# A streaming encoder layer: projecting all tiles first, and mixing with the output projection between its steps

## What is computed

```python
def trunk_layer(x, c, S0, k_cache, v_cache, lb, ...):
    mod = jnp.dot(jax.nn.silu(c), w_ada) + b_ada              # 9 rows of 6 x 1024
    sh1, sc1, g1, sh2, sc2, g2 = [m[:, None, :] for m in jnp.split(mod, 6, axis=-1)]
    h = rmsnorm(x, ln1) * (1 + sc1) + sh1
    qa, ka, va, qb, fb, ib, gb = jnp.split(jnp.dot(h, w_in), SPLITS, axis=-1)
    # widths 512, 128, 128, 512, 512, 512, 512
    # A: QK norm per head, windowed attention (8 heads, 2 key heads) with sinks and ALiBi -> oa
    # B: HGRN2 recurrence over blocks, 8 heads of a 64 x 64 state:
    #    logf = log sigmoid(z), k = sigmoid(-z), b = cumsum(logf)
    #    o = tril((q k) exp(b_t - b_s)) i + (q exp(b)) S,  S' = exp(b_last) S + (k exp(b_last - b))^T i
    ob = rmsnorm(ob, o_norm) * jax.nn.silu(gb)
    x = x + g1 * jnp.dot(jnp.concatenate([oa, ob], axis=-1), w_out)
    h2 = rmsnorm(x, ln2) * (1 + sc2) + sh2
    x = x + g2 * moe(h2, ...)                                 # 16 experts, top 2
```

## Time and profile before

| | us |
|---|---|
| median of 3 runs (lowest, highest) | 1480.14 (1477.21, 1480.64) |
| the profiled execution's own time | 1478.23 |
| its span | 1476.5 |
| PE busy in the span | 1276.9 |
| DVE, ACT, POOL busy | 771.5, 545.0, 264.5 |
| mean granted PE clock | 0.914 |

### The profile page before, as it was taken

How to read it: one execution, slowest core, us unless ns; L and a number is a source line. 1 busy time by engine, 2 the same in 40 slices (tenths; PEclk the granted TensorE clock), 3 DMA queues, 4 the chain that set the end, 5 groups by cost and what they waited for, 6 DMA issues and landing times. The chain is left out here.

```text
span 1476.5 us, 21409 instructions
## 1 busy us (share of the span) xinstructions
PE 1276.9 (86%) x6661; PEld 919.6 (62%) x6662; DVE 771.5 (52%) x1187; ACT 545.0 (37%) x916; POOL 264.5 (18%) x287
## 2 busy tenths in 40 slices
PE   5529999999999999994969973699999999969964
PEld 0014666665766666564648863588888787858853
DVE  0010656466475655647244446555528665865752
ACT  0011535435253443524143330444416444644540
POOL 1000101102010110204000000233133233323313
PEclk7759999999999999995779995799999999989988
DMA  9970000000000000005273328458667979898874
GB/s 355 415 286 11 5 15 0 14 0 14 14 0 14 0 14 0 14 2 130 38 202 124 118 100 291 151 182 273 215 184 250 332 256 309 300 309 253 266 281 85
DMA packets 87921, 215.01 MB, mean 146 GB/s; under 512 B 16577, under 2 KB 20289, under 8 KB 84818
## 3 DMA queue, kind: packets, MB, share of 16 engines
q1 hardware_dynamic: 75794, 170.58, 32.3%
q0 software_dynamic: 12096, 44.05, 11.4%
HBM read 188.31 MB, written 26.23 MB: 145 GB/s over the span
## 5 line engine op out<-in xcount | busy, mean ns | idle before, releaser
L481 PE MATMUL psum<-w_in_sb,x_res 128*128 128x512 f32 (+1 forms) x864 | 353.2, 563 | 4.4 <-DVE x_res L471 4.4
L481 PEld LDWEIGHTS psum<-w_in_sb,x_res 128*128 128x128 f32 x864 | 160.9, 191 | 164.1 <-issue 156.8
L1942 PE MATMUL psum<-e_w_h,e_x_h 128*128 128x512 f32 x432 | 174.9, 405 | 29.5 <-DVE w_gu L2055 23.1
L1943 PE MATMUL psum<-w_gu,e_x_h 128*128 x432 | 171.8, 398 | 0.0
L1944 PE MATMUL psum<-e_w_h,e_x_l 128*128 128x512 f32 x432 | 171.6, 397 | 0.0
L2055 DVE TENSOR_TENSOR w_gu<-w_gu,e_w_h 128x1024 f32 x128 | 146.7, 1220 | 20.5 <-ACT e_w_h L1996 20.5
L1996 ACT ACTIVATE e_w_h<-w_gu 128x1024 fp32r x128 | 123.0, 1048 | 53.9 <-issue 33.0
L1889 POOL DMA_INDIRECT out<-e_work,e_to x26 | 87.6, 3371 | 302.3 <-DVE e_work L2043 302.3
L1942 PEld LDWEIGHTS psum<-e_w_h,e_x_h 128*128 128x128 f32 x432 | 83.4, 193 | 47.9 <-DVE w_gu L2055 23.6
L1944 PEld LDWEIGHTS psum<-e_w_h,e_x_l 128*128 128x128 f32 x432 | 83.3, 193 | 18.2
L1943 PEld LDWEIGHTS psum<-w_gu,e_x_h 128*128 128x128 f32 x432 | 83.4, 193 | 17.0
(11 more groups left out here) (393 smaller groups left out, 2055.9 us busy)
## 6 DMA issues: line engine op xcount, KB each, us to landing
w_gu<-in_w_e_gate SPq DMA_DIRECT2D x16, 2048.0 KB, 11.0
w_gu<-in_w_e_up SPq DMA_DIRECT2D x16, 2048.0 KB, 15.8
w_dn<-in_w_e_down SPq DMA_DIRECT2D x16, 2048.0 KB, 15.2
stage<-in_w_ada SPq DMA_DIRECT2D x24, 1024.0 KB, 13.2
x_res<-in_x SPq DMA_DIRECT2D x20, 512.0 KB, 3.7
w_in_sb<-in_w_in SPq DMA_DIRECT2D x5, 2048.0 KB, 19.0
out<-r_x SPq DMA_DIRECT2D x9, 512.0 KB, 2.6
h_d<-r_h SPq DMA_DIRECT2D x9, 512.0 KB, 2.9
```

Source lines behind the costliest of these rows:

```text
L481: last = pe.matmul(psum[:, PJ0 + j % 2, 0:n], h_t[:, k, :], b["w_in_sb"][:, k, a:a + n], start=(k == 0), stop=(k == KC - 1))
L1942: pe.matmul(psum[:, j, :], x_h[:, k, :], wh, start=(k == 0), stop=False)
L1943: pe.matmul(psum[:, j, :], x_h[:, k, :], wl, start=False, stop=False)
```

## The change

The stages become projection, sampling, mixing, routing, experts; `output` is gone as a stage.

**Projection** makes h for all nine tiles, split in a high and a low part (`h_h`, `h_l`) that stay in SBUF, and walks over `w_in` by column group, each group loaded and split once (ACT high, DVE low, two slots), for all tiles. A job is one group for one tile, 24 fp32r products; for f and q the weights are the stationary operand, so the result comes out with features on partitions, 128 features by 384 rows a job. The elementwise work follows each job and the results go to memory (`feat` 9.4 MB: running sum, log key less running sum, key, query; `tok` 8.3 MB: i, gate, q, k, v). `w_ada` chunks 8 to 23 are loaded and used between jobs.

```diff
+GROUPS = (("i", CIB, QW), ("f", CFB, QW), ("q", CQB, QW), ("kv", CK, 2 * KW), ("qa", CQ, QW), ("g", CGB, QW))
+BY_WEIGHT = ("f", "q")
+JOBS = [(g, n) for g, (name, _, _) in enumerate(GROUPS) for n in range(4 * NCH if name in BY_WEIGHT else NT)]
+BANKS = 4
+STAGES = 3
+TOK_RING = 3
...
+            for n, (g, i) in enumerate(JOBS):
...
+                if name == "i":
+                    if i + 1 < NT:
+                        turn_x(i + 1)
+                    pe.wait_ge(s["hl_ready"], i + 1)
...
+                    if name in BY_WEIGHT:
...
+                        pe.matmul(out, wh, h_h[:, k, at], start=(k == 0), stop=False)
+                        pe.matmul(out, wl, h_h[:, k, at], start=False, stop=False)
+                        last = pe.matmul(out, wh, h_l[:, k, at], start=False, stop=(k == KC - 1))
...
+                if name in BY_WEIGHT and i < KC:
...
+                    ada(chunk)
+            def load_x(t):
+                if t >= 2:
+                    sp.wait_ge(s["x_turned"], t - 1)
...
+                if name == "i":
+                    if i + 2 < NT:
+                        load_x(i + 2)
```

**Sampling** comes before the mixing, reads the ninth tile from memory, and loads and splits `w_out`:

```diff
+            for kv in range(NKV):
+                sp.dma_start(w_raw[kv * HD:(kv + 1) * HD, 0:G, :],
...
+            sp.dma_start(w_raw[:, G:KC, :], d["w_out"][QW:2 * QW, :]...
...
+            def split(ks):
+                act.wait_ge(s["w_out_loaded"], 3 * 16)
+                for k in ks:
+                    a(w_oh[:, k, :], w_raw[:, k, :], ACT.Copy).then_inc(s["wh_ready"], 1)
...
             act.wait_ge(s["kgap_ready"], 1)
             a(k_d[:, :], k_d[:, :], ACT.Exp).then_inc(s["kexp_ready"], 1)
+            split(range(0, 2))
             act.wait_ge(s["top_ready"], 2)
```

**Mixing** is an unrolled loop over eight tiles, which loads each tile's `feat` and `tok` (double-buffered). POOL makes the gaps:

```diff
+                pool.tensor_tensor(g[:, :, 0, :], e[:, :, 0, :], mid, ALU.add)
+                pool.tensor_tensor(g[:, :, 1, :], c[:, :, 1, :], mid, ALU.subtract).then_inc(s["gap_ready"], 1)
...
+                pool.tensor_tensor(xw[:, :], x2[:, u % 2, :], table_row(2, u), ALU.mult).then_inc(s["xw_ready"], 1)
```

PE's order has six fp32r products of the output projection of the tile before (`fill`) in the places of the projection:

```diff
+                fill(t, 0)
+                scores(t, 0)
+                level(t, 0)
+                if t:
+                    turn_ob(t - 1)
+                fill(t, 1)
+                level(t, 1)
+                if t:
+                    pe.wait_ge(s["mixb_ready"], t)
+                    turn_h2(t - 1)
+                fill(t, 2)
+                level(t, 2)
+                turn_probs(t, 0)
+                if t:
+                    logits(t - 1)
+                fill(t, 3)
+                values(t, 0)
+                scores(t, 1)
+                level(t, 3)
+                fill(t, 4)
+                level(t, 4)
+                fill(t, 5)
+                turn_probs(t, 1)
+                level(t, 5)
+                fill(t, 6)
+                values(t, 1)
+                level(t, 6)
...
+                fill(t, 7)
```

More of the change, by code:

```diff
@@ L935, in sampling @@
+OUT_A, OUT_B, M0, M1, M2, M3, PJ0, PJ1 = range(8)
+def sampling(nc, b, d, sinks, cache_k, cache_v, state_in, s_sample):
+    psum, ident, mix_s = b["psum"], b["ident"], b["mix_p"][:, 1, :, :]
     KS = WIN + L
@@ new lines, in mixing @@
+        v_sb = sb("v_sb", [P, 2, KW])
+        dist = sb("dist", [P, 2, 2 * P])
+        sink = sb("sink", [P, NKV * G])
+        score = sb("score", [P, G, 2 * P])
+        p_t = sb("p_t", [P, 2 * G, P])
+        top_s, neg_top, sink_e = (sb(n, [P, G]) for n in ("top_s", "neg_top", "sink_e"))
+        den, rec = sb("den", [P, NKV, G]), sb("rec", [P, NKV, G])
+        o_a = sb("o_a", [P, G, NKV, HD])
+        exp_b, q_e, k_d, kd_tok = (sb(n, [P, QW]) for n in ("exp_b", "q_e", "k_d", "kd_tok"))
@@ L1387, in _ @@
[L1387 to L1396 removed]
+            load_tile(1)
@@ new lines, in level @@
+            def level(t, i):
+                n = t * NL + i
+                pe.wait_ge(s["lv_ready"], n + 1)
+                if i == 0:
+                    pe.wait_ge(s["pair_clear"], t + 1)
+                else:
+                    pe.wait_ge(s["pair_ready"], n)
+                for h in range(8):
+                    r = slice((h % 2) * HD, (h % 2 + 1) * HD)
+                    c = h // 2
+                    last = pe.matmul(psum[:, M0 + h % 2, c * HD:(c + 1) * HD], gap[r, n % GAPS, c * P:(c + 1) * P],
+                                     q_l[r, i % 2, c * HD:(c + 1) * HD], start=True, stop=True)
+                    if h >= 6:
+                        last.then_inc(s["lv_mm"], 1)
@@ L1453, in _ @@
+            u = NU - 1
+            for k in range(4):
+                fill(u, k)
+            turn_ob(TP - 1)
+            pe.wait_ge(s["mixb_ready"], TP)
+            turn_h2(u - 1)
+            for k in range(4, KC):
+                fill(u, k)
+            logits(u - 1)
+            pe.wait_ge(s["logit_ready"], u)
+            turn_h2(u)
+            logits(u)
         @block.scalar
@@ new lines, in place @@
+            def place(t, i):
+                h = LEVELS[i]
+                dve.wait_ge(s["lv_mm"], 2 * (t * NL + i + 1))
+                alone(dve)
+                for a in range(2):
+                    out = pair[:, a, :, :].rearrange("p e (n two h) -> p e n two h", two=2, h=h)[:, :, :, 1, :]
+                    m = bc(b["level_mask"][:, i, :].rearrange("p (n h) -> p n h", h=h).bitcast(I32), 1, 4)
+                    src = psum[:, M0 + a, 0:4 * HD].rearrange("p (e n h) -> p e n h", e=4, h=h)
+                    last = dve.copy_predicated(out, m, src)
+                last.then_inc(s["pair_ready"], 1)
```

1852 lines of the change are left out of this document (933 added, 919 removed).

## The result

The changed kernel takes 1498.85 us (median of 4 runs, 1493.82 to 1502.9) against 1479.58 for the kernel before in the same session: a ratio of 1.0131, with an interval of 1.0097 to 1.0165. It is slower by 19.3 us. The forecast said 7.6 slower, 1486, in a range from 1450 to 1545.

A forecast was written before the change was run, and what follows sets the result against it. PE was taken as the limit in the largest part before routing; projection 364, sampling to 456, load 10.7, eight tiles of 51 and tail 33 put routing at 901.2 against 893.6: +7.6, 1486 us, range 1450 to 1545.

The forecast's parts named there:

- The 384-column products: Projection groups f and q: 24 jobs of 24 products, taken at 0.174 us each, 100 us in all.
- The rival of a pass that doesn't stream: Projection: narrow fp32r products cost more, or loads and stores hold PE; +20 to +60, 1506 to 1546; chance 0.10.
- The new wait: Sampling: splits wait for `w_out` loads, in at 36 us, first level at 41; 15 us more, stage 92.
- The rival with `w_out` in time: Sampling stays at 77 us: −15, 1471 mostly, 1465 to 1485; chance 0.10.
- The first load: Between sampling and mixing: the first mixing tile waits for features and token rows, 8 to 12 us, taken 10.7.
- T: Mixing tile period: 46.9 + 1 + 3.2 = 51 us; below 50.0 faster, a rival put at 0.30.
- 8.3 of waits: Mixing tile: PE waits at the border, level 1's placing and the second exponentials, 8.3 us together.
- 1 of collisions: Mixing tile: DVE held by POOL, about one collision of 0.73 us in each of two chains; bounds 0 and 10.2.
- a spell costs half its length: 1.6 to 3.4; I take two spells at the shorter: Mixing tile: PE drops to half clock behind waits; two spells cost 3.2 us; bounds none, or three at 3.4.
- The rival built on it: Mixing: every wait starts PE cold, three spells of 3.4 us; T 57 or more, +56, 1534; chance 0.12.
- The tail: After the eighth mixing tile: eight fills, two h2 turns, logits, last residual and norm; 33 us.

The follow-up runs named there:

- The run with late splits: Changed kernel with sampling's first two splits of the output weight moved behind the softmax, together with the next ones: 1476.22 us, ratio 0.9972.
- the last run: The packed order with the router's logits products placed one by one between the products of fill 3: 1378.37 us, ratio 0.9309.
- the calm tile with two waits gone: Tile at clock 1.00 in changed kernel with second scores ahead of first values, their maximum ahead of placing level 3, level 0's placing ahead of first maximum: 1431.49 us.
- the run with all edits: Changed kernel with scores and maximum moved earlier, level 0's placing earlier, attention output turned early at the border, and sampling's splits behind the softmax: 1424.53 us, ratio 0.9591.
- the packed order: Changed kernel with early border turn, sampling's splits behind the softmax, and tile order rewritten so PE has work wherever it waited: 1389.09 us, ratio 0.941.
- scores first: Changed kernel with second half's scores ahead of first half's values on PE, and its maximum ahead of placing level 3 on DVE: 1447.52 us, ratio 0.9785.
- the second exponentials' wait filled: Changed kernel with eight useless 128x512 products in PE's wait for the second exponentials alone: 1476.28 us, ratio 0.9983.

## Why the prediction was right, and where it was not

**Stages.** Forecast for the ends of projection, sampling and mixing: 364, 456, 901.2. Measured 369.1, 465.7 and 915.0. The projection's terms hold one by one: first job 45.4 (44), group i 69.6 (68.5), f and q with their chunks 119.3 (117), kv 26.2 (26), qa and g 98.3 (98), drain 10.3 (10). The 384-column products, which no row had priced, start 0.173 us apart in their trios (0.174 taken). The rival of a pass that doesn't stream is out.

**Sampling.** The new wait was found from SP's order, and the terms were short by 4 us: the loads landed 40 us behind the stage's start (36), level 0 came at 45 (41), the stage took 96.6 (92). The run with late splits shows that this wait was the stage's whole excess: 75.2 without it. The rival with `w_out` in time is out. What I did not see is how cheap the cure of this wait was.

**The first load** took 8.7 of the 10.7, counted from the stage's border.

**The tile.** T was forecast at 51 and is 51.5, but this is not one success: two errors of some 3 us cancel, and that is luck. The forecast had 38.6 of PE's own work, 8.3 of waits, 1 of collisions and 3.2 of clock. Measured: PE idle 6.4 and busy 45.0. Its own work is 38.1 in the last run and 38.9 in the calm tile with two waits gone, both at clock 1.00, so 6.1 to 6.9 are half clock. The waits were oversized by 1.9 and, with the collisions in them, by 2.9; the clock was undersized by 2.9 to 3.7. The places of the waits were right: level 1 for the placing (2.0, forecast 3.3), the second exponentials (2.3, forecast 2.4), the border (2.2, forecast 2.0 and 0.5).

**The step that failed** is "a spell costs half its length: 1.6 to 3.4; I take two spells at the shorter". Their number was nearly right (14 in six tiles, 2.3 a tile). Their length was not: the shorter was 3.2 us, and here a spell lasts 3 to 14 us, 6.6 on average (a clock of 0.85 over 308.8 us is 92 us at half clock), and 20 in the run with all edits. The longer kind was already in the trace of before. In sampling PE was busy 16.35 of 17.1 us with small products, and the clock stayed at half; the prediction names this stretch among the rivals and does not price it:

```profile
707.90:725.00 17.10, 16.35 (x74) 10.29 (x74) 2.69 (x5) 0.60 (x1) 1.69 (x2) 0.50 0.00 1
```

The Trainium skill (TensorE: Matmul & The Clock Gate, HAM oscillation) tells of bursts that all start cold behind their waits, which are waits for loads of some 3 to 5 us; these are 2.1 to 2.3. By this trace it is nearly so, 14 of 18. The rival built on it (0.12) had the mechanism right, three spells a tile where there were 2.3, and 3.4 us for one where the tile's 6.1 to 6.9 make 2.6 to 3.0; its T of 57 was too high by that and by the oversized waits. It deserved more than it got. Waits are not all of it: in the packed order the clock also fell with no wait, at the row of logits.

**Collisions.** The term was 1. Beside POOL level 1's queries take 0.78 where they take 0.42 alone, and the small sums 0.5 to 0.7 in place of 0.16; if two of these stand on the path, it is some 0.7, an estimate. Biased scores, which read PSUM, kept between 0.405 and 0.421 us in all 64 cases. That agrees with the Trainium skill (SBUF — State Buffer, Who interferes with whom): of DVE's instructions in the mixing only those with two SBUF inputs were clearly slowed. The upper end of 10.2 was far too high.

**The tail.** From the eighth tile's turns to the routing it is 88.9 us; 51 and 33 were forecast, 4.9 short, with the clock at 0.77 in it. No experiment looked at this part.

**The sum.** +5.1 in the projection, +4.6 in sampling, −2.0 in the load, +6.1 in mixing (of which 4.9 in the tail): 13.8 later than forecast at the routing. The sign, slower, came out as the likeliest single outcome, and T against 50 was the right question for the loop: mended in order, it needs 38.6 and the change wins.

## What to carry to other kernels

When dense work is cut up to fill the gaps of a chain of small steps, write PE's order so that it has something at every wait of even 1 to 2 us. Here two waits of 2.0 and 2.3 us, taken away one at a time, gave 5.4 and 7.3 us a tile, and 8.9 together, over half of it behind the waits. If no real work fits, useless products in the gap were better than the gap in all three runs that had them. Where the clock falls with no wait, look for a row of very narrow products and mix it with wide ones: that cured it here, though the same row did no harm in other orders. And when a split of late-arriving weights is put on ACT or DVE, ask what stands behind it in program order: the same instructions a few lines later were worth 21 us.

## What the runs showed of the hardware that I had not expected

- Identical tiles took 41.2 and 52.3 us in one execution, because the clock fell behind a wait of 1.3 us in one and not in the other (and for 3 us more behind a wait of 1.6 us). A single tile's time is no measure of such an order.
- The wait of some 2 us at level 1 was followed by no fall in six tiles of one order (scores first) and by one in each of six tiles of another (the second exponentials' wait filled).
- TensorE stayed at 1.2 GHz for 20 us (733 to 753 in the run with all edits) while the profile had it busy in every microsecond, with fills of six wide products among the small steps.
- The clock fell with no wait at all, within a microsecond of the end of 1.96 us of products with 16 columns, in four of six tiles of one order. In the other orders the same row had no fall behind it in these tiles.
- A DVE product of 128x256 took 1.66 us in place of 0.42 beside a POOL product of 128x1024.
